# Layer 0's feed-forward: modulation chunks beside the down products only, the first product copied to a place of its own, gate times up and its remainder on GpSimd

## The reference

```
def conv_ffn(h, w_gate, w_up, conv_w, conv_b, w_down):
    g = h @ w_gate                                    # 1024 -> 2816
    g = conv over 3 neighbouring tokens of g + conv_b
    return (jax.nn.silu(g) * (h @ w_up)) @ w_down     # 2816 -> 1024

def modulation(cond, w_mod, b_mod):                   # 1024 -> 6 * 1024, for the next block
    return jnp.split(jax.nn.silu(cond) @ w_mod + b_mod, 6, axis=-1)
```

## Time and profile before

| | us |
|---|---|
| median of 3 runs (2810.42 to 2814.7) | 2812.66 |
| the profiled execution | 2806.88 |
| its span | 2805.1 |
| TensorE busy (96% of the span) | 2683.8 |
| VectorE busy (54%) | 1509.0 |
| ScalarE busy (38%) | 1068.9 |
| GpSimd busy (8%) | 219.3 |
| the Winograd stage with down groups 1 to 4, from 547.7 to 1037.3 | 489.6 |

### The profile page before, as it was taken

One profiled execution on the slowest core, in us unless ns is written; L12 is line 12 of the kernel. 1 busy time (PEld: TensorE's weight loads), 2 busy tenths in 40 slices (PEclk: granted clock), 3 DMA queues, 4 the chain that ended last, 5 costly groups with the idle time before them and its releaser, 6 DMA issues.

```text
span 2805.1 us, 43405 instructions
## 1 busy us (share of the span) xinstructions
PE 2683.8 (96%) x18096; PEld 2259.5 (81%) x18096; DVE 1509.0 (54%) x2714; ACT 1068.9 (38%) x1797; POOL 219.3 (8%) x161
## 2 busy tenths in 40 slices
PE   7999999999999999998999999999989999999999
PEld 5876778888889887886888888888766888888887
DVE  3377544765565565427847646459558344433333
ACT  3355543432232244635735323342156222322221
POOL 2000000222122120204001001100000000000000
PEclk9999999999999999999999999999989999999999
DMA  6232010122323331220012332222210232222322
GB/s 264 102 114 75 24 38 31 61 98 99 128 98 121 121 105 40 82 68 16 1 61 68 106 99 97 90 69 76 96 67 9 98 98 97 84 90 86 106 88 88
DMA packets 65633, 235.71 MB, mean 84 GB/s; under 512 B 7200, under 2 KB 9376, under 8 KB 64800
## 3 DMA queue, kind: packets, MB, share of 16 engines
q1 hardware_dynamic: 65152, 231.38, 24.2%
q10 hardware_dynamic: 288, 1.57, 0.2%
HBM read 230.82 MB, written 2.10 MB: 83 GB/s over the span
## 4 chain that ended last, share of the span: by engine, by line
PE 78%; DVE 11%; ACT 4%; issue 2%; DMA 2%; POOL 2%; SPq 0%; ACTq 0%; DVEq 0%
PE PSA L847 74%; DVE WS L2729 3%; DMA W<-in_weights 2%; PE PSA L1162 2%; ACT WS L2017 1%; POOL W L2632 1%; PE PSA L1299 1%; POOL W L2625 1%; PE PSA L1556 1%; DVE H L3416 1%; DVE Y L3018 1%; DVE stat L3664 1%; DVE Y L3059 1%; DMA Y<-in_early 1%; ACT Y L2235 1%
## 5 line engine op out<-in xcount | busy, mean ns | idle before, releaser
L847 PE MATMUL PSA<-HS,WS 128*128 128x512 f32 (+1 forms) x4656 | 979.2, 370 | 14.2 <-DVE HS L2898 7.2
L847 PEld LDWEIGHTS PSA<-HS,WS 128*128 128x128 f32 x4656 | 811.4, 190 | 170.5 <-issue 9.7
L2729 DVE TENSOR_TENSOR WS<-W,WS 128x1024 fp32r<-128x1024 f32 (+4 forms) x420 | 412.6, 995 | 505.1 <-ACT WS L2017 504.7
L2017 ACT ACTIVATE WS<-W 128x1024 fp32r<-128x1024 f32 (+4 forms) x420 | 347.0, 844 | 668.7 <-PE PSA L847 351.0
L847 PE MATMUL PSA<-YS,WS 128*128 128x512 f32 x2280 | 480.8, 371 | 3.5 <-DVE YS L3688 3.5
L847 PEld LDWEIGHTS PSA<-YS,WS 128*128 128x128 f32 x2280 | 400.5, 188 | 81.6 <-DVE YS L3688 3.9
L847 PE MATMUL PSA<-Y 128*64 128x128 f32 (+9 forms) x2112 | 220.5, 322 | 16.1 <-ACT Y L2170 6.5
L847 PEld LDWEIGHTS PSA<-Y 128*64 128x64 f32 (+3 forms) x2112 | 143.1, 147 | 69.8 <-issue 46.3
L1299 PE MATMUL PSA<-YS,WS 128*128 128x384 f32 x912 | 165.2, 335 | 0.2
L1299 PE MATMUL PSA<-HS,WS 128*128 128x384 f32 x684 | 137.1, 354 | 26.8 <-ACT Y L2290 23.5
L1299 PEld LDWEIGHTS PSA<-YS,WS 128*128 128x128 f32 x912 | 158.5, 188 | 1.3 <-issue 1.3
(11 more groups left out here) (380 smaller groups left out, 2904.1 us busy)
## 6 DMA issues: line engine op xcount, KB each, us to landing
W<-in_weights SPq DMA_DIRECT2D x397, 512.0 KB, 3.5
Y<-in_early SPq DMA_DIRECT2D x4, 2048.0 KB, 18.8
W<-in_weights SPq DMA_DIRECT2D x16, 256.0 KB, 2.7
X<-in_x SPq DMA_DIRECT2D x4, 768.0 KB, 20.2
W<-in_weights SPq DMA_DIRECT2D x16, 128.0 KB, 2.2
Y<-in_ssm ACTq DMA_DIRECT2D x1, 1024.0 KB, 6.3
out<-X SPq DMA_DIRECT2D x1, 1024.0 KB, 4.4
C<-in_consts SPq DMA_DIRECT2D x1, 884.5 KB, 30.7
```

Source lines behind the costliest of these rows:

```text
L847: return pe.matmul(out, lhsT, rhs, start=first, stop=last)
L2017: act.activation(dst, w, ACT.Copy).then_inc(weights_rounded, 1)
L2729: tt(rest, w, rounded.bitcast(F32), ALU.subtract).then_inc(weights_split, 1)
```

## The change

Modulation steps leave the tiles and stand only beside the down products, behind output tiles d = 0 to 5 of each group, two chunks each (before: one chunk in each of the 19 tiles, between p7 and p2, and two, two, two and one behind d = 0, 2, 4 and 6). The number of chunks stays; the steps with chunks go from 35 to 24. ScalarE's copy of p1 goes to FIRST, a place of its own in the free part of the input's buffer, and stands ahead of the roundings of that point. Each left operand is rounded and split one product earlier relative to its slot, in the same order. `make_hidden` and `hidden_rest` of tiles 3 to 21 go from VectorE to GpSimd, where they stand ahead of the weight sums of the tile two later. Where scaling of the gate and a rounding stand at the same point (p3), the rounding now comes first. At the end the last down group's first three output tiles wait for u2 of tile 21 instead of c21.

The diff, without the declarations and the new homes of the last group's weights:

```diff
 def mod1_steps():
     sizes = [(("ffn", 1), 1)]
-    for m in range(FIRST_WINO, MF):
-        sizes.append((("ffn", m), 1))
-        if group_after(m):
-            sizes += [(("down", group_after(m), d), 2 if d < 6 else 1) for d in (0, 2, 4, 6)]
+    for g in range(1, LAST_G):
+        sizes += [(("down", g, d), 1 if g == LAST_G - 1 and d == 5 else 2) for d in range(6)]
...
         if g is None:
-            due[m, "p7"], due[m, "p2"] = ("wb", m + 1, "p5"), ("wb", m + 1, "p6")
...
+            for p, q in zip(PRODUCTS[1:], PRODUCTS):
+                due[m, p] = ("wb", m + 1, q)
...
         else:
-            due[m, "p6"], due[m, "p7"] = ("db", g, 0), ("db", g, 1)
...
+            for p, i in zip(PRODUCTS[1:5], range(4)):
+                due[m, p] = ("db", g, i)
...
                     for p in PRODUCTS:
                         wino_product(m, p)
-                        if p == "p7":
-                            all_drained(3)
-                            modulation(("ffn", m), 4)
...
                         down_part(("down", 0, g, d), g, d, (2, 1, 0)[d % 3], range(4), ALL)
                         if ("down", g, d) in m_index:
+                            all_drained(3)
                             modulation(("down", g, d), 4)
...
-                    pe.wait_ge(outputs_summed, value("outputs_summed", (MF - 1, "c21")))
+                    pe.wait_ge(outputs_summed, value("outputs_summed", (MF - 1, "u2")))
...
+                    if p == "p1":
+                        act.wait_ge(products_done, value("products_done", (m, "p1")))
+                        if m > FIRST_WINO:
+                            act.wait_ge(outputs_summed, value("outputs_summed", (m - 1, "u2")))
+                        act.activation(FIRST, bank(m, "p1").rearrange("p (a b) -> p a b", b=P), ACT.Copy)\
+                            .then_inc(first_copied, one("first_copied", m))
                     after = item if kind == "db" else item[1:]
                     if after in due:
                         weights_up_to(due[after])
...
+            def make_hidden(m):
+                pool.wait_ge(gate_ready, value("gate_ready", (0, m)))
+                pool.wait_ge(outputs_summed, value("outputs_summed", (m, "c21")))
+                gc, a = GC[:, m % 2, :], hidden_parts(m)
+                pool.tensor_tensor(gc, gc, UP, ALU.mult).then_inc(hidden_made, one("hidden_made", m))
+                pool.wait_ge(input_rounded, value("input_rounded", ("ff", 0, m)))
+                pool.tensor_tensor(a[:, 1, :], gc, a[:, 0, :].bitcast(F32), ALU.subtract)\
+                    .then_inc(hidden_ready, one("hidden_ready", m))
             for m in range(FIRST_WINO, MF):
+                if m - 2 >= FIRST_WINO:
+                    make_hidden(m - 2)
                 for s in ("s1", "s2", "s3", "s4"):
                     weight_sum(m, s)
+            for m in (MF - 2, MF - 1):
+                make_hidden(m)
...
-                        summed(m, "u2", UP1, bank(m, "p6"), UP1, "p6")
+                        u2, p6 = (v.rearrange("p (a b) -> p a b", b=P) for v in (UP1, bank(m, "p6")))
+                        summed(m, "u2", u2, p6, FIRST, "p6")
...
-                    elif p == "p2":
-                        ring_modulation(("ffn", m))
...
-                    if p == "p4":
-                        make_hidden(m)
-                    elif p == "p1" and m > FIRST_WINO:
-                        hidden_rest(m - 1)
```

More of the change, by code:

```diff
@@ L112, in wino_chunks @@
             continue
-        for c in range(4 if g else 2):
-            w.append(("down", 0, g, c))
-            w += [("mod", 1, n) for n in mods.get(("down", g, 2 * c), ())]
+        for what in ((0, 1) if g == 0 else (0, 1, "m0", "m1", 2, "m2", 3, "m3", "m4", "m5")):
+            if what in range(4):
+                w.append(("down", 0, g, what))
+            else:
+                w += [("mod", 1, n) for n in mods["down", g, int(what[1])]]
     return w + [("down", 0, LAST_G, c) for c in range(4)]
@@ L314, in build @@
         hidden_made = sem("hidden_made")
+        hidden_ready = sem("hidden_ready")
         weights_summed = sem("weights_summed")
@@ L500, in build @@
         for m in range(KD):
-            HOMES["db", LAST_G, m] = HT2[:, :, 0:4, N2 + P * m:N2 + P * m + P] if m < 3 else \
-                part(YS, (6144, 7168, 8192, 9216, 10240)[m - 3], 2, 4, P)
-        FREED_HOME = {0: "p1", 1: "p1", 2: "p1", 3: "p5", 4: "p5", 5: "p5", 6: "p6", 7: "p6"}
+            HOMES["db", LAST_G, m] = HT2[:, :, 0:4, N2 + P * m:N2 + P * m + P] if m < 2 else \
+                part(YS, (11264, 6144, 7168, 8192, 9216, 10240)[m - 2], 2, 4, P)
+        FREED_HOME = {0: "p1", 1: "p1", 2: "p6", 3: "p5", 4: "p5", 5: "p5", 6: "p6", 7: "p6"}
         for m in range(3, KD):
@@ L533, in build @@
         UP1, UP2 = UP[:, 0:N2], UP[:, N2:T]
+        FIRST = HT32[:, 0, 0:3, T - P:T]
         HF = part(Y, 12288, KD, T)
@@ L611, in hidden_parts, with hidden_split @@
             return part(YS, 2 * T * (m % 4), 2, T)
+        def hidden_split(eng, m):
+            if m < FIRST_WINO:
+                eng.wait_ge(activated, value("activated", (0, m)))
+            else:
+                eng.wait_ge(hidden_ready, value("hidden_ready", m))
         def bank(m, p):
@@ L2010, in round_weights @@
                     if item in HOMES:
-                        last = (FIRST_WINO if item[2] < 3 else MF - 1, FREED_HOME[item[2]])
+                        last = (FIRST_WINO if item[2] < 2 else MF - 1, FREED_HOME[item[2]])
                         act.wait_ge(products_done, value("products_done", last))
@@ L2283, in wino_forward @@
                         weights_up_to(due[after])
-                    if p == "p4":
+                    if p == "p3":
+                        begin_gate(m)
+                    elif p == "p4":
                         end_gate(m)
-                    elif p == "p1":
-                        if m > FIRST_WINO:
-                            round_hidden(m - 1)
-                        act.wait_ge(products_done, value("products_done", (m, "p1")))
-                        act.activation(UP1, bank(m, "p1"), ACT.Copy).then_inc(first_copied, one("first_copied", m))
+                    elif p == "p1" and m > FIRST_WINO:
+                        round_hidden(m - 1)
                 round_hidden(MF - 1)
@@ L3031, in make_hidden @@
                     gc, up = GC[:, m % 2, :], ("up", 0, m)
-                    if m < FIRST_WINO:
-                        dve.wait_ge(psum_filled[slot(up)], turn(up))
-                        tt(gc, gc, PS[slot(up)][:, 0:T], ALU.mult).then_inc(psum_drained[slot(up)], 1)
-                    else:
-                        dve.wait_ge(outputs_summed, value("outputs_summed", (m, "c21")))
-                        tt(gc, gc, UP, ALU.mult).then_inc(hidden_made, one("hidden_made", m))
+                    dve.wait_ge(psum_filled[slot(up)], turn(up))
+                    tt(gc, gc, PS[slot(up)][:, 0:T], ALU.mult).then_inc(psum_drained[slot(up)], 1)
                 def hidden_rest(m):
```

20 lines of the change are left out of this document (9 added, 11 removed).

## The result

The changed kernel takes 2868.17 us (median of 4 runs, 2865.23 to 2869.38), the kernel before in the same session 2811.54 (4 runs, 2808.08 to 2814.7). The ratio is 1.0201, with a 95% interval of 1.0185 to 1.0218: 2.0% slower. The prediction was 2856 with a range of 2830 to 2884. The profiled execution took 2867.17 us, its span 2865.4, so the span is 60.3 us longer than before.

What follows compares the result with a forecast made beforehand. TensorE, busy for 96% of the span, was taken as the bound. Groups +50.5, tiles -11.1, stage's end -1.5 and clock +6 gave +43.9: 2850.8 us profiled, 2856 as median; range 2830 to 2884.

Steps and rivals of the forecast that it cites:

- The wait in the groups: Down groups: TensorE waits 1.85 us for VectorE's copy behind the drain, five times a group, 37.0 us in all.
- rival 4: Down groups: the move costs no wait because VectorE's copy gets through in time; 2813 us, no change; chance 0.06.
- The modulation in the groups: Down groups: with all modulation chunks there and no waits, the four groups would take 169.9 us.
- The clock: TensorE's granted clock falls behind four of the twenty new waits, 1.4 us each, about +6 us; ends 0 and 28.
- Rival 2: Clock falls behind nearly every new wait: 28 us for 6, and some in the tiles; 2882 us; chance 0.15.
- The chain in the tiles: Tiles: p3 to the next tile's p3 through GpSimd's product, remainder and s1 takes 17.35 us, over 14.56 of matmuls.
- the hold: Tiles: VectorE instructions with two SBUF inputs and GpSimd ones reading SBUF exclude each other; twice 0.55, 1.1 us per chain.
- The first tile's p3: First tile of sets 2 to 5: c22 is there 14.55 us after the start, where p3 could begin after 10.40.
- The tiles together: All nineteen tiles in five sets take 322.1 us for 333.2, so -11.1.
- rival 1: GpSimd and VectorE don't hold each other in these shapes; tiles give 29 us for 11; 2838 us; chance 0.15.
- Rival 3: Tiles: chain through GpSimd is covered, tiles run at TensorE's pace; price 45.5 us; 2805 us, faster; chance 0.04.
- The copy of p1: Tiles: TensorE's 23.5 us of waits for ScalarE's copy go; what is late next is p3, waiting for c22.

Runs made afterwards that it cites:

- the run with the place alone: Kernel before, with only p1's copy made first at its point and into a place of its own: 2813.45 us, ratio 1.0.
- both edits: Changed kernel with modulation steps closed by VectorE before the drain, and product and remainder back on VectorE: 2771.63 us, ratio 0.9846 to the kernel before.
- split behind c22: Changed kernel, but VectorE takes the remainder of p5's weights behind u3 and c22, not between u2 and u3: 2843.72 us, ratio 1.0102.
- release first: Changed kernel, but in the down groups VectorE closes a modulation step before the next output tile's drain: 2815.2 us, ratio 0.9993.
- release between: Changed kernel, but VectorE closes the modulation step between the drain's two instructions: 2853.95 us, ratio 1.014.

## Why the prediction was right

**The wait in the groups**: right in mechanism and nearly in size. The twenty waits stand where the prediction put them, released by the copy to MT. One costs 1.97 us, predicted 1.85; twenty 39.4 for 37.0. Removing what makes them wait removes them all, so rival 4 (no wait) falls.

**The modulation in the groups**: without waits the groups took 170.8, predicted 169.9.

**The clock**: the term that was mis-sized. It was +6, four slow output tiles at 1.4; nine at 1.5 make 13.6, and the slow products in the tiles, for which the sum has no term, make 9.4 more. The earlier trace rows show one wait with a fall behind it and one without. The trace of before has thirteen waits for the copy: five with a fall behind them (four of 2.29 to 2.33 and one of 1.87) and eight without (1.12 to 1.84). The fall behind the shortest of the five:

```profile
1011.42 6.00 PE L1299 MATMUL PSA<-HS,WS 128*128 128x384 f32 x24 [1.87 <-ACT Y L2290]
```

So waits of 1.85 could fall on either side, and the choice of four was no more than a guess between 0 and 20. Rival 2 (nearly every one) was further off in the groups, 28 for 13.6, but it alone looked for falls in the tiles; its time, 2882, is about as far off as the forecast's on the other side. The slow tiles in the groups vanish with the waits.

**The chain in the tiles**: 16.88 us for 17.35, in the order that was summed. Term by term from the rows above: p3 to the silu's end 7.28 (predicted 7.30), product 1.93 with its handover (1.95), rounding 0.88 (0.83), remainder 1.92 (1.95), s1 1.70 with the hold (1.83), rounding of p5 0.72 (0.62), its split 1.26 (1.23), u3 and c22 with p3's start 1.19 (1.21); the 0.42 of handovers was counted beside durations that already overlap by some of it. The first tile's p3 came at 683.55 - 669.32 = 14.23 us, predicted 14.55. The waits of p3 in the later tiles of a set were called nearly 3 us; they are 1.3 to 2.0.

The tiles together are 324.2 for 322.1, and that they agree so well is luck. Without the six slow products they would be about 314.8 (324.2 less 9.4, an estimate; behind a slow product the next p3 comes after 18.2 to 19.0 us instead of 16.88). The sum had the nine chains 0.5 too long each, the first tiles 0.3 to 0.5 and the ends 0.4; these 7 us made up for the clock that it left out. Without the hold its own terms give 305, not 304. The hold between VectorE and GpSimd is there, which rival 1 denied: 1.54, 1.92 and 1.22 us beside 0.68. The Trainium skill's rule ("SBUF — State Buffer", Who interferes with whom) agrees with these rows. Rival 3 (tiles at TensorE's pace) falls with the 16.88. The run with product and remainder on VectorE comes near its price, 41.7 us for 45.5, though the 9.4 of the clock are among the 41.7.

**The copy of p1**: right that its waits go and that p3 is late next. What the prediction didn't ask is whether the copy was the cause of the earlier trace rows; by the run with the place alone it wasn't.

**The sum.** 2850.8 was predicted for the profiled execution, it took 2867.17: 10.9 from the groups (2.4 the wait, 7.6 the clock, 0.9 the steps), 2.2 from the tiles, 3.4 from outside the stage, where the parts before and behind it were 1.6 and 1.8 us longer. This is inside the scatter of the eleven profiled kernels, whose code there is nearly the same: the stage begins at 546.5 to 549.7, and the part behind the last group's first output tile takes 1755.9 to 1762.2 us. The forecast of 2856 for the median also took over the 5.8 us by which one execution of the kernel before lay under its median; here that distance is 1.0, so it hid a part of the miss.

**Where a gain was to be had.** Modulation in the groups and roundings one product earlier belong together: the roundings without the move cost 39 us, the move without them (with both edits) gained 19 over the kernel before, both 43. The change lost this by two orders: release behind the drain, 53 us, and the product on GpSimd, 42.

## What to carry to other kernels

When a step moves nearer to the one that feeds it, look at where the release stands in the other engine's order: a short instruction that somebody waits for goes ahead of a longer one that must wait itself. Element work that is moved to a lightly used engine is costed as a chain from one tile to the next, not by that engine's busy share: GpSimd was busy for 10% of the span, and yet it set the pace of the tiles. And the releaser that a list of waits names may be the last link of a chain; take the chain back two or three steps before paying for a cure of the last one. Where the old trace shows the clock falling behind waits, every wait of that length in the new order is charged for it, not only the waits that the change adds.

## What the runs showed of the hardware

- TensorE's clock behind short waits. Behind a wait of 1.73 us and the modulation step's small matmuls, nine of twenty output tiles ran partly at the lower level (granted clock 0.74 over one of them), in three kernels alike (the change, product and remainder on VectorE, split behind c22); with 1.33 us five of twenty; with none, none. In the tiles, with products of 384 columns on both sides, three kernels with the same order there (the change, release first, release between) have 39 waits: behind 3.43 to 3.67 us all twelve next products were slow, behind 2.31 the only one, behind 2.01 to 2.04 eight of sixteen, behind 1.25 to 1.94 none of ten. In the run with the place alone products were slow behind 1.77 and 1.86 too (3.12 and 3.90 us), so these counts give no length that decides.
- A GpSimd operation with two SBUF inputs of 128x768 takes 1.85 us, VectorE's 0.95. Where such operations of the two engines meet, the one that starts later ends only after the other: VectorE's split of 0.68 takes 1.92 beside the remainder and ends 0.55 after it, and GpSimd's s1 of 1.28 takes 1.74 behind that split.
